# Two-layer encoder step: the even layer's input tiles from split rows and weights, its long convolution divided between VectorE with PSUM and GpSimd

## The reference, cut to what matters

```python
proj = h @ w_in                     # h: 640 x 1024 after RMSNorm
a_val, a_gate, z, xbc, dt_raw = split(proj)        # 512, 512, 512, 1024, 8 columns
a_glu = a_val * sigmoid(a_gate)
a_conv = causal_dwconv(a_glu, conf_state, conf_w, conf_b)     # width 31, 512 channels
a_out = silu(layernorm(a_conv))
xbc_c = silu(causal_dwconv(xbc, ssd_conv_state, xbc_w, xbc_b))  # width 4, 1024 channels
...                                 # step sizes from dt_raw, SSD scan over xbc_c, gate silu(z), RMSNorm
out = concat([a_out, b_out]) @ w_out
```

## Time and profile before

| what | before |
|---|---|
| time, median of 3 runs | 1737.92 us (1737.47 to 1738.1) |
| span of the profiled execution | 1735.7 us |
| PE busy | 1702.0 us, 98% |
| DVE busy | 1058.7 us, 61% |
| ACT busy | 683.9 us, 39% |
| POOL busy | 370.5 us, 21% |
| granted TensorE clock over the span | 1.000, its upper level (2.4 GHz) |

### The profile page before, as it was taken

The page is one execution under the profiler, slowest core; times in us unless marked ns, Lnnn a source line. Parts: engine busy times, 40 slices in busy tenths (PEclk is TensorE's granted clock), DMA queues, the critical chain, the costliest instruction groups (busy, mean ns, idle before and its releaser), DMA issues.

```text
span 1735.7 us, 27688 instructions
## 1 busy us (share of the span) xinstructions
PE 1702.0 (98%) x11360; PEld 1543.0 (89%) x11360; DVE 1058.7 (61%) x1717; ACT 683.9 (39%) x1219; POOL 370.5 (21%) x289
## 2 busy tenths in 40 slices
PE   7999998999999999999999999999999999999999
PEld 6566556797999999999989899789899999999999
DVE  3699867637667647465654424744676774655574
ACT  4111243435525525253552124633543453544352
POOL 3012100211104324132213132200110241414240
PEclk9999999999999999999999999999999999999999
DMA  8222330142303131403143221603320313122212
GB/s 263 101 77 103 93 107 28 49 195 98 104 27 138 32 130 46 135 19 128 31 141 74 75 73 64 246 27 114 153 93 25 128 48 115 61 70 86 87 66 91
DMA packets 39674, 162.30 MB, mean 94 GB/s; under 512 B 9384, under 2 KB 10280, under 8 KB 25600
## 3 DMA queue, kind: packets, MB, share of 16 engines
q1 hardware_dynamic: 32240, 124.59, 21.5%
q0 software_dynamic: 7312, 35.98, 5.8%
HBM read 149.87 MB, written 10.42 MB: 92 GB/s over the span
## 4 chain that ended last, share of the span: by engine, by line
PE 92%; DVE 5%; ACT 2%; issue 1%; DMA 0%; POOL 0%; SPq 0%; DVEq 0%; ACTq 0%
PE G L940 68%; PE S L940 11%; PE Q L940 11%; PE Q L1635 1%; ACT work L1731 0%; DVE rstd L2344 0%; DMA ring<-in_w_mk 0%; DVE ev_low L2593 0%; ACT rstd L1731 0%; DVE stats L2623 0%; DVE resid L2875 0%; ACT h_split L1731 0%; PE Q L1347 0%; DVE stats L2992 0%; DVE work L2636 0%
## 5 line engine op out<-in xcount | busy, mean ns | idle before, releaser
L940 PE MATMUL G<-ffn_rows,w_split 128*128 128x320 f32 x2160 | 329.8, 309 | 0.0
L940 PEld LDWEIGHTS G<-ffn_rows,w_split 128*128 128x128 f32 x2160 | 320.1, 188 | 0.0
L1731 ACT ACTIVATE w_split<-ring 128x512 fp32r<-128x512 f32 (+2 forms) x224 | 159.1, 711 | 316.8 <-PE G L940 208.4
L940 PE MATMUL G<-front,ring 128*128 128x128 f32 (+2 forms) x832 | 223.3, 430 | 11.0 <-DMA ring<-in_w_mk 9.3
L940 PEld LDWEIGHTS G<-front,ring 128*128 128x128 f32 x832 | 133.0, 193 | 100.0 <-issue 95.9
L856 POOL TENSOR_TENSOR mkT<-ring 128x512 f32<-128x512 f32 x72 | 98.2, 1369 | 564.6 <-DMA ring<-in_w_up 382.2
L940 PE MATMUL G<-h_split,w_split 128*128 128x320 f32 x1344 | 200.9, 310 | 1.2 <-DVE w_split L2359 0.8
L940 PEld LDWEIGHTS G<-h_split,w_split 128*128 128x128 f32 x1344 | 197.5, 188 | 1.9 <-issue 1.3
L940 PE MATMUL G<-g_split,w_split 128*128 128x320 f32 x1056 | 163.7, 310 | 0.1
L940 PEld LDWEIGHTS G<-g_split,w_split 128*128 128x128 f32 x1056 | 156.7, 188 | 1.7 <-DVE w_split L2848 1.4
L2715 DVE TENSOR_TENSOR w_split<-ring,w_split 128x512 fp32r<-128x512 f32 (+1 forms) x124 | 105.8, 854 | 59.9 <-ACT w_split L1731 58.7
(11 more groups left out here) (351 smaller groups left out, 2818.8 us busy)
## 6 DMA issues: line engine op xcount, KB each, us to landing
ring<-in_w_up SPq DMA_DIRECT2D x44, 1024.0 KB, 4.8
ring<-in_w_down SPq DMA_DIRECT2D x48, 256.0 KB, 2.6
ring<-in_w_down SPq DMA_DIRECT2D x32, 320.0 KB, 2.9
front<-in_mem_k POOLq DMA_DIRECT2D x8, 1024.0 KB, 6.1
front<-in_mem_v POOLq DMA_DIRECT2D x8, 1024.0 KB, 10.6
ring<-in_w_mk SPq DMA_DIRECT2D x4, 1024.0 KB, 5.9
ring<-in_w_mv SPq DMA_DIRECT2D x4, 1024.0 KB, 10.9
ring<-in_w_glu SPq DMA_DIRECT2D x4, 1024.0 KB, 8.6
```

What stands on the lines that cost most here:

```text
L940: return nc.tensor.matmul(out, lhsT, rhs, start=start, stop=stop, **kw)
L1731: return nc.scalar.activation(*a, **k)
```

## The change

1. The first pair of glu tiles stays fp32; the narrow tile's matmuls stand between the first tile's blocks (`first_pair`). The other 18 input tiles, numbered `i` = 0 to 17 (0 to 5 glu, 6 to 13 xbc, 14 to 17 z), are made by `input_product` from split rows and weights.
2. The high rows are written by ScalarE over `x`, the low rows by VectorE over `h`; SyncE loads `x` from memory again after the last z tile, and VectorE waits for it ahead of the cross attention's part of the program.
3. For each of the 18 tiles ScalarE writes the high weights (`input_high`, into one of four buffers) and VectorE the low ones, over the ring slot (`input_low`).
4. VectorE's taps cover the prompt only, with the partial sum in PSUM (`S`), and each waits for the one directly before it. The streams' taps are on GpSimd: `request_taps`, 31 products and 30 sums of 128 frames for each channel block.
5. `conv_sum` moves behind the first two xbc blocks' convolutions and waits for GpSimd's taps too.

```diff
 
+IN_GLU, IN_XBC = 6, 14
+IN_TILES = IN_XBC + 4
+def in_tile(i):
+    if i < IN_GLU:
+        return TILE0["glu"] + 2 + i
+    return xbc_tile(i - IN_GLU) if i < IN_XBC else z_tile(i - IN_XBC)
+def in_slot(i):
...
+        def in_piece(i):
+            name, at = ("glu", i + 2) if i < IN_GLU else ("xbc", i - IN_GLU) if i < IN_XBC else ("z", i - IN_XBC)
+            slot = (CHUNK[name] + at // 2) % RING
+            src, lo = (w[:, slot, :].rearrange("p (k n) -> p k n", k=KD)[:, :, at % 2 * P:(at % 2 + 1) * P]
+                       for w in (ring, ring_r))
+            return src, in_w[in_slot(i)][:, :, :], lo
+        in_rows = [x_r, ev_lo]
...
+                if c == CHUNK["evout"] + 3:
+                    tile_wait(sp, z_tile(3))
+                    for k in range(0, KD, 2):
+                        sp.dma_start(x[:, k:k + 2, :], dram["x"][:, k:k + 2, :]).then_inc(x_again, 16)
...
+            def request_taps(j):
+                out = runs(acc[:, j, SEQ:T])
+                base = made[0]
+                def product(w):
+                    if w > 3:
+                        pool.wait_ge(taps_made, base + 2 * (w - 3) + 1 + (w - 3 < CW - 1))
+                    nc.gpsimd.tensor_scalar(runs(tap_room[:, w % 3, :]), padded(aglu, j, 0, CPROMPT, CREQ, w)[1],
+                                            pr("cw", j * CW + w), 1.0, ALU.mult, ALU.mult).then_inc(taps_made, 1)
+                nc.gpsimd.tensor_scalar(out, padded(aglu, j, 0, CPROMPT, CREQ, 0)[1], pr("cw", j * CW), pr("cb", j),
+                                        ALU.mult, ALU.add).then_inc(taps_made, 1)
+                product(1)
+                for w in range(1, CW):
+                    if w + 1 < CW:
+                        product(w + 1)
+                    pool.wait_ge(taps_made, base + 2 * w)
+                    nc.gpsimd.tensor_tensor(out, out, runs(tap_room[:, w % 3, :]), ALU.add).then_inc(taps_made, 1)
+                made[0] += 2 * CW - 1
             memory_keys(0)
             pool.wait_ge(pads_in, 16 * 12)
             for j in range(4):
+                if j == 2:
+                    memory_keys(1)
                 read_wait(pool, TILE0["glu"] + 2 * j + 1)
                 store(dram["o_conf_p"][:, j], aglu[:, j, SEQ:SEQ + CW - 1], early=True)
                 store(dram["o_conf_s"][:, j], aglu[:, j, CPROMPT:].rearrange(
                     "p (r t) -> p r t", r=REQ)[:, :, STEP:], early=True)
-
-            memory_keys(1)
+                request_taps(j)
...
+            def input_product(i, halfway=None):
+                n = in_tile(i)
+                begin(n)
+                out = GF[n % 2]
+                pe.wait_ge(in_split, i + 1)
+                weights = [in_piece(i)[1], in_piece(i)[2]]
+                for k in range(KD):
+                    if i == 0:
+                        pe.wait_ge(in_lo, k + 1)
+                    for wpart, xpart in ((0, 0), (0, 1), (1, 0)):
+                        for f in range(2):
+                            fr = slice(f * HT, (f + 1) * HT)
+                            m = mm(out[:, fr], weights[wpart][:, k, :], in_rows[xpart][:, k, fr],
+                                   k == 0 and wpart + xpart == 0, k == KD - 1 and wpart == 1)
+                    if halfway is not None and k == KD // 2 - 1:
+                        m.then_inc(halfway, 1)
+                m.then_inc(tile_done, 1)
...
+            def first_pair():
+                n = TILE0["glu"]
...
+                for k in range(KD):
+                    pe.wait_ge(applied, APPLIED["mix0"] - KD + 1 + k)
+                    q, o = k % 4, PAR["wdt"][0] + k * NH
+                    strip, w = slice(32 * q, 32 * q + 32), par[:, o:o + 32]
+                    mm(steps[strip, 0:512], w, h[:, k, 0:512], k < 4, k >= 4, tile_position=(0, 32 * q))
+                    m = mm(steps[strip, 512:T], w, h[:, k, 512:T], k < 4, k >= 4, tile_position=(0, 32 * q))
+                    if k == KD - 1:
+                        m.then_inc(tile_done, 1)
+                    w = ring[:, s, k * 256:k * 256 + P]
+                    mm(gate[:, 0:512], w, h[:, k, 0:512], k == 0, k == KD - 1)
+                    m = mm(gate[:, 512:T], w, h[:, k, 512:T], k == 0, k == KD - 1)
+                m.then_inc(tile_done, 1)
+                begin(n + 1)
+                for k in range(KD):
+                    w = ring[:, s, k * 256 + P:k * 256 + 2 * P]
+                    mm(value[:, 0:512], w, h[:, k, 0:512], k == 0, k == KD - 1)
+                    m = mm(value[:, 512:T], w, h[:, k, 512:T], k == 0, k == KD - 1)
+                    m.then_inc(h_used if k < KD - 1 else tile_done, 1)
...
-            projections("glu", 8, KD, rows(h), norm="mix0")
-            narrow(TILE0["dtp"], "wdt", h)
+            first_pair()
+            for i in range(IN_GLU):
+                input_product(i)
...
+            for k in range(KD):
+                act.wait_ge(applied, APPLIED["mix0"] - KD + 1 + k)
+                A(x_r[:, k, :], h[:, k, :], ACT.Copy).then_inc(in_hi, 1)
...
+            def input_high(i):
+                user = in_slot_user(i)
+                if user >= 0:
+                    tile_wait(act, in_tile(user))
+                src, hi, _ = in_piece(i)
+                name, at = ("glu", i + 2) if i < IN_GLU else ("xbc", i - IN_GLU) if i < IN_XBC else ("z", i - IN_XBC)
+                chunk_wait(act, CHUNK[name] + at // 2)
+                A(hi, src, ACT.Copy).then_inc(in_high, 1)
...
+                tile_wait(act, t0 + 2 * j)
+                A(tmp[:, j % 2, :], glu_out(t0 + 2 * j), ACT.Sigmoid).then_inc(read[(t0 + 2 * j) % 2], 1)
+                if j < 2:
+                    input_high(2 + 2 * j)
+                    input_high(3 + 2 * j)
...
+            for m2 in range(2):
+                input_high(IN_GLU + 2 * m2)
+                input_high(IN_GLU + 2 * m2 + 1)
+                memory_values(1, m2)
...
-            for j in range(6):
+            for j in range(4):
                 xbc_rows(j)
-            for j in range(2):
-                xbc_silu(j)
+                input_high(IN_GLU + 4 + j)
+            xbc_silu(0)
+            xbc_rows(4)
+            xbc_silu(1)
+            xbc_rows(5)
...
             xbc_rows(6)
+            input_high(IN_XBC)
...
             xbc_rows(7)
+            input_high(IN_XBC + 1)
             z_gate(0)
-            xbc_silu(4)
+            input_high(IN_XBC + 2)
...
                 for at in range(taps_done[0], taps_done[0] + count):
-                    j, w, i = at // (2 * CW), at % (2 * CW) // 2, at % 2
-                    out = (acc[:, j, 0:SEQ], runs(acc[:, j, SEQ:T]))[i]
-                    src = padded(aglu, j, 0, CPROMPT, CREQ, w)[i]
+                    j, w = at // CW, at % CW
+                    part = S[:, j % 2, :]
+                    src = padded(aglu, j, 0, CPROMPT, CREQ, w)[0]
                     tap = pr("cw", j * CW + w)
                     if w == 0:
-                        ins = v.tensor_scalar(out, src, tap, pr("cb", j), ALU.mult, ALU.add)
+                        ins = v.tensor_scalar(part, src, tap, pr("cb", j), ALU.mult, ALU.add)
                     else:
-                        dve.wait_ge(conv, at - 1)
-                        ins = v.scalar_tensor_tensor(out=out, in0=src, scalar=tap, in1=out,
-                                                     op0=ALU.mult, op1=ALU.add)
+                        dve.wait_ge(conv, at)
+                        ins = v.scalar_tensor_tensor(out=part if w < CW - 1 else acc[:, j, 0:SEQ], in0=src, scalar=tap,
+                                                     in1=part, op0=ALU.mult, op1=ALU.add)
                     ins.then_inc(conv, 1)
                 taps_done[0] += count
 
+            def input_low(count):
+                for i in range(split_done[0], split_done[0] + count):
+                    dve.wait_ge(in_high, i + 1)
+                    src, hi, lo = in_piece(i)
+                    v.tensor_tensor(lo, src, hi.bitcast(F32), ALU.subtract).then_inc(in_split, 1)
+                split_done[0] += count
+            def input_low_rows():
+                for k in range(KD):
+                    dve.wait_ge(in_hi, k + 1)
...
+                    v.tensor_tensor(ev_lo[:, k, :], h[:, k, :], x_r[:, k, :].bitcast(F32), ALU.subtract)\
+                        .then_inc(in_lo, 1)
...
+            input_low(2)
+            input_low_rows()
...
-                conv_taps(32 if j < 3 else 44)
+                if j == 0:
+                    input_low(2)
+                conv_taps(9)
+                if j in (1, 2):
+                    input_low(1)
+                conv_taps(8)
+            input_low(2)
             step_sizes()
-            conv_taps(8 * CW - taps_done[0])
+            conv_taps(14)
+            input_low(2)
+            conv_taps(27)
+            input_low(1)
+            conv_taps(8)
+            input_low(1)
+            conv_taps(4 * CW - taps_done[0])
...
+            def taps_sum():
```

(63 more changed lines are left out.)

30 lines of the change are left out of this document (22 added, 8 removed).

## The result

The changed kernel takes 1745.8 us (median of 4 runs, 1744.64 to 1747.75) against 1737.99 of the kernel before on the same chip: ratio 1.0047, 95% interval 1.0035 to 1.0060. It is 7.8 us slower, where 6.9 us faster was forecast. The span of its profiled execution is 1743.8 us.

What follows compares the result with a forecast made beforehand. TensorE, busy 98% of the span, bounds the kernel, and VectorE would set the pace after the change. Sum: 28.6 us gained, less 19.9 of waits and 2.0 for GpSimd's interference, is 6.7, giving 1731 us; range 1717 to 1746.

Steps and rivals of the forecast that it cites:

- The narrow tile is only moved ... 2.5 us: First pair on TensorE: the narrow tile's matmuls keep their earlier price of 2.5 us, so the pair ends at 67.5.
- The waits: TensorE waiting for VectorE at tile 5, the statistic, tile 12 and tile 15: 7.2, 7.7, 3.7 and 1.3 us, 19.9 together.
- just in time: Tile 11: VectorE's low weights ready at 183.7 us, due at 184.3, so no wait of TensorE was counted.
- the port: GpSimd slowing VectorE's low weights by 0.2 us each, 2.0 in all; as a rival 0.53 each, 1734.5 us, chance 0.08.
- its own sign of being wrong: End of the input tiles: the prediction called itself wrong if the last z tile ended after 258 us.
- The split tiles: TensorE's 18 input tiles: 7.06 us each as fp32r instead of 8.65 as fp32, 28.6 us less.
- Fed in time: Case that VectorE never makes TensorE wait: 1709 us, needing taps under 0.6 us, left to the tail.
- The taps: VectorE's prompt taps, partial sum in PSUM: mean near 750 ns, starts 0.79 us apart, all 124 taking 98 us.
- Cheap and dear taps: Rivals on VectorE's taps: 0.65 to 0.73 us each, 1722 at 0.70, chance 0.22; 0.85 each, 1737, chance 0.10.
- GpSimd, right by the rows: GpSimd's request taps: 0.31 and 0.43 us per instruction, 25 us a block, hidden with 7 us to spare before VectorE's sum.
- GpSimd too late: Rival: GpSimd's taps at 1.07 us hold up the memory keys and VectorE's sum, 7 us slower, 1745, chance 0.20.

Runs made afterwards that it cites:

- Experiments 1 and 2: The changed kernel with the first pair's narrow matmuls in two groups of four blocks: 1737.67 us; in four groups of two blocks: 1740.59 us.
- experiment 3: The changed kernel with narrow matmuls in two groups, plus 44 unread matmuls in TensorE's wait ahead of tile 5: 1734.67 us, 3.0 less than without them.
- few_taps: The changed kernel with narrow matmuls in two groups, only 11 of 31 prompt taps and one request tap computed: 1712.21 us.
- experiment 5: The changed kernel with only one of 31 request taps on GpSimd, the others left out: 1741.68 us, 4.1 less than the changed kernel.

## Why the prediction was wrong

- **"The narrow tile is only moved ... 2.5 us": the step that failed.** Set one by one between wide blocks, the narrow pairs cost 2.47 - 1.08 = 1.39 us each, 11.1 for all, not 2.5. Experiments 1 and 2 show it: 8.1 us in the time. The row that I took the 2.5 from had four strips side by side, and I kept its price for an order in which they can't be. The Trainium skill, TensorEngine Tiling (Array Packing), section Key Properties, states both halves: tiles of the array run in parallel, and a change of the tiling mode drains it. The first is what these rows show; the second no run here separates.
- **The waits, right in size.** 7.2, 7.7, 3.7 and 1.3 us were predicted (19.9 in all); 7.4, 9.3, 2.2 and 0.8 were measured (19.7), at tile 5, the statistic, tile 12 and tile 15. A fifth, 0.55 at tile 11, stood in the sum as just in time. The measured 20.2 also hold what was priced apart as the port (2.0), so they stand against 21.9.
- **Their price, mis-sized.** I counted a wait at its own length. Behind two of them the clock was at 1.2 GHz. At tile 5 that cost 3.0 us (experiment 3), which passed on because VectorE waited for this tile. Behind the statistic's wait its matmuls took 2.50 instead of 1.24 us and tile 12 8.57 instead of 7.04, 2.8 us by the rows. Of these the statistic's 1.26 is hidden: TensorE waits 2.2 us right behind it for low weights that VectorE makes without waiting for the statistic. What the 1.5 us at tile 12 cost wasn't tested by itself.
- **The balance.** By the prediction the last z tile ends at 258.75 - 6.7 = 252.05; it ended at 265.88, 13.8 later (its own sign of being wrong was an end after 258). By the rows: the first pair starts 0.5 later and takes 28.2 instead of 19.8, 8.4 more; the slow clock is 2.8 at tile 5 and 2.8 behind the statistic's wait; the waits are 1.7 less than the 21.9. That makes 12.8; the last 1.0 isn't assigned.
- **The split tiles, right.** A pair of matmuls every 0.293 us makes 7.04 a tile, 7.06 predicted. Fed in time, the kernel was to take 1709, and few_taps took 1712.2.
- **The taps, right.** 755 ns, 16 in 12.6 us, so 0.79 apart. By the estimate from the Trainium skill (VectorE: DVE Perf Modes, The TRN2 errata) a tap from PSUM would cost 65 ns more; at most 16 appeared: 755 ns in PSUM, 739 to 748 in SBUF with GpSimd idle. Cheap and dear taps both fell.
- **GpSimd, right by the rows.** 0.37 and 0.45 us for 0.31 and 0.43, done 5.8 us ahead of the sum. That the taps in PSUM don't feel it was right; the rest was charged at 2.0 us and came to 4.1 (experiment 5), with slower first operations of the xbc convolution in it (606 ns against 535 without GpSimd's taps). What I didn't see is that the sum's place in PSUM protects GpSimd more than VectorE.
- **The sign.** The measured time is that of the rival "GpSimd too late" (1745), but by another mechanism, so its chance was no insight. That 1745.8 lies inside the stated range of 1717 to 1746 is luck for the same reason.

## What to carry to other kernels

Matmuls narrower than the array are cheap only next to others on different strips: moving one costs what its new neighbours make it cost. Behind a wait of many us on TensorE comes a stretch at the slow clock (here behind those of 3.5, 7.4 and 9.3 us), so in the sum such a wait gets a second term, unless another wait right behind it hides it, and work that nobody reads is a cheap test of it. What a faster tile is worth is read from the engine that sets the pace: only the time that it had waited for this tile comes back. When an engine's work gets faster, the written order of its helpers has to be made anew: here the same instructions took 1745.8, 1733.4, 1740.0 and 1727.1 us in four of the orders tried.

## What I had not expected of the hardware

- A narrow group costs 1.2 us with one, two or four strips filled.
- VectorE's taps with both inputs in SBUF slow GpSimd's instructions from 0.37 and 0.45 to 0.80 and 0.83 us (medians), while they themselves go only from 755 to 797 ns.
- 44 matmuls whose result nobody reads, put into a wait, made the kernel 3.0 us faster.
